# Moving two kinds of low-part subtraction from VectorE to GpSimd in the retention heads of an encoder kernel

## The reference, cut to what matters

```
h  = rmsnorm(x);  z = h @ w_in
y_ret = retention(rq, rk, rv, rg) @ w_ret_o        # 4 heads, dk 128, dv 256, both directions
   o = o * rsqrt(mean(o*o));  o = o * norm_g;  out = silu(g) * o
y_dil = dilated_attention(dq, dk, dv) @ w_dil_o    # 3 groups x 4 heads
x = x + (sigmoid(g_ret) * y_ret + sigmoid(g_dil) * y_dil) @ w_out
```

## Time and profile before

| | us |
|---|---|
| median of 3 runs (2579.22 to 2579.46) | 2579.38 |
| the profiled execution | 2579.25 |
| its span in the profile | 2577.4 |
| PE busy | 2569.2 |
| DVE busy | 1936.7 |
| ACT busy | 1120.5 |
| POOL busy | 128.3 |

### The profile page before, as it was taken

The page is one execution under the profiler, slowest core; times in us unless marked ns, Lnnn a source line. Parts: engine busy times, 40 slices in busy tenths (PEclk is TensorE's granted clock), DMA queues, the critical chain, the costliest instruction groups (busy, mean ns, idle before and its releaser), DMA issues.

```text
span 2577.4 us, 36835 instructions
## 1 busy us (share of the span) xinstructions
PE 2569.2 (100%) x14577; PEld 2255.8 (88%) x14577; DVE 1936.7 (75%) x2430; ACT 1120.5 (43%) x1369; POOL 128.3 (5%) x199
## 2 busy tenths in 40 slices
PE   9999999999999999999999999999999999999999
PEld 7999988888888888999989999888888888889998
DVE  8877866886776679777788777677867766797776
ACT  5433444445555234333443334444455542343332
POOL 1111000110001000000000000011100000000000
PEclk9999999999999999999999999999999999999999
DMA  5433245545443433333223332454554434333331
GB/s 183 149 124 119 66 142 192 174 159 175 138 138 115 163 101 120 101 103 98 99 83 123 98 98 74 174 177 147 172 155 138 138 126 153 115 115 98 102 107 53
DMA packets 201202, 328.98 MB, mean 128 GB/s; under 512 B 15572, under 2 KB 122497, under 8 KB 200525
## 3 DMA queue, kind: packets, MB, share of 16 engines
q1 hardware_dynamic: 186312, 286.35, 34.8%
q0 software_dynamic: 14112, 36.50, 3.9%
q10 hardware_dynamic: 646, 4.31, 0.4%
HBM read 289.11 MB, written 42.64 MB: 129 GB/s over the span
## 4 chain that ended last, share of the span: by engine, by line
PE 99%; DVE 1%; ACT 0%; DMA 0%; issue 0%; ACTq 0%
PE proj L692 23%; PE proj L694 23%; PE proj L693 23%; PE acc L692 9%; PE acc L693 9%; PE acc L694 9%; PE acc L1062 1%; PE acc L988 0%; PE acc L1011 0%; PE acc L970 0%; PE acc L971 0%; PE acc L1001 0%; PE acc L972 0%; PE acc L1000 0%; PE acc L765 0%; PE acc L759 0%
## 5 line engine op out<-in xcount | busy, mean ns | idle before, releaser
L692 PE MATMUL proj<-h_hi,ring_hi 128*128 128x256 f32 (+1 forms) x1632 | 553.4, 339 | 0.9 <-DVE h_lo L1788 0.8
L694 PE MATMUL proj<-h_hi,ring_lo 128*128 128x256 f32 (+1 forms) x1632 | 544.6, 334 | 0.0
L693 PE MATMUL proj<-h_lo,ring_hi 128*128 128x256 f32 (+1 forms) x1632 | 543.7, 333 | 0.0
L692 PE MATMUL proj<-y_hi,ring_hi 128*128 128x256 f32 (+1 forms) x1472 | 450.5, 306 | 0.0
L694 PE MATMUL proj<-y_hi,ring_lo 128*128 128x256 f32 (+1 forms) x1472 | 450.5, 306 | 0.0
L693 PE MATMUL proj<-y_lo,ring_hi 128*128 128x256 f32 (+1 forms) x1472 | 450.5, 306 | 0.0
L1262 ACT ACTIVATE ring_hi<-raw 128x1024 fp32r<-128x1024 f32 (+1 forms) x175 | 209.9, 1203 | 360.7 <-PE acc L694 194.6
L694 PEld LDWEIGHTS proj<-h_hi,ring_lo 128*128 128x128 f32 x1632 | 309.9, 190 | 31.2
L692 PEld LDWEIGHTS proj<-h_hi,ring_hi 128*128 128x128 f32 x1632 | 310.3, 190 | 30.3 <-DVE ring_lo L2569 1.2
L693 PEld LDWEIGHTS proj<-h_lo,ring_hi 128*128 128x128 f32 x1632 | 310.4, 190 | 27.5
L694 PEld LDWEIGHTS proj<-y_hi,ring_lo 128*128 128x128 f32 x1472 | 281.2, 191 | 12.5
(11 more groups left out here) (335 smaller groups left out, 4310.5 us busy)
## 6 DMA issues: line engine op xcount, KB each, us to landing
raw<-in_w_in SPq DMA_DIRECT2D x120, 512.0 KB, 4.7
raw<-in_ffn_gate SPq DMA_DIRECT2D x88, 512.0 KB, 3.7
raw<-in_ffn_up SPq DMA_DIRECT2D x88, 512.0 KB, 4.3
raw<-in_ffn_down SPq DMA_DIRECT2D x56, 512.0 KB, 4.4
qkv_d<-work POOLq DMA_DIRECT2D x72, 256.0 KB, 2.6
work<-in_ffn_down SPq DMA_DIRECT2D x32, 512.0 KB, 5.7
xs<-qkv_d SPq DMA_DIRECT2D x24, 512.0 KB, 6.3
xs<-in_w_in SPq DMA_DIRECT2D x16, 512.0 KB, 5.2
```

What stands on the lines that cost most here:

```text
L692: pe.matmul(o, s_hi, m_hi, start=start, stop=False, skip_group_check=onto)
L693: pe.matmul(o, s_hi, m_lo, start=False, stop=False, skip_group_check=onto)
L694: return pe.matmul(o, s_lo, m_hi, start=False, stop=stop, skip_group_check=onto)
```

## The change

GpSimd's program for a head gets three instructions between its fourth store and the wait for the squares: for n > 0 the two subtractions of `ret_low` of the head before, and for every n the low part of unit `at(4)`. VectorE loses the same instructions. VectorE's next weight splits (`at(1)` of heads 1 to 3 and `M_R0` in the merge) get a wait for GpSimd's increment of `weights_lo`, to keep the count in order.

```diff
@@ gpsimd head(l, n), behind the four stores of sigmoid tiles
+                if n:
+                    for e in (0, 1):
+                        pool.wait_ge(ret_hi, 2 * H - 1 + e)
+                        pool.tensor_tensor(y_lo[:, ds(2 * n - 2 + e, 1), :], ret_og[e].unsqueeze(1),
+                                           y_hi[:, ds(2 * n - 2 + e, 1), :].bitcast(fp32), ALU.subtract).then_inc(ret_lo, 1)
+                u = unit(l, HEAD_BASE + HEAD_UNITS * (n + 1))
+                pool.wait_ge(weights_hi, u.index + 1)
+                pool.wait_ge(weights_lo, u.index + LO_CREDIT)
+                pool.tensor_tensor(w_lo[u.slot], raw[:, u.slot, :], w_hi[u.slot].bitcast(fp32), ALU.subtract).then_inc(weights_lo, 1)
                 pool.wait_ge(ret_o_read, 4 * H + 2)
@@ vector
-            def split(u, n=2048):
+            def split(u, n=2048, behind_pool=False):
                 dve.wait_ge(weights_hi, u.index + 1)
+                if behind_pool:
+                    dve.wait_ge(weights_lo, u.index + LO_CREDIT)
                 dve.tensor_tensor(w_lo[u.slot][:, 0:n], raw[:, u.slot, 0:n], w_hi[u.slot][:, 0:n].bitcast(fp32),
                                   ALU.subtract).then_inc(weights_lo, 1)
@@ vector heads(l, n), n > 0
-                    split(at(1))
+                    split(at(1), behind_pool=True)
@@
                 reduce(3)
-                if n:
-                    ret_low(H - 1, n - 1)
                 ret_decay(H, 2)
@@
                 reduce(5)
-                split(at(4))
                 ret_decay(H, 3)
@@ vector merge(l)
-                split(at(M_R0))
+                split(at(M_R0), behind_pool=True)
```

## The result

The changed kernel takes 2589.19 us, median of 6 runs (2588.91 to 2589.38); the kernel before, beside it on the same chip, 2579.3 us (2579.17 to 2579.53). The ratio is 1.0038, 95% interval 1.0028 to 1.0049: slower by 9.9 us. 2590.0 had been forecast.

What follows compares the result with a forecast made beforehand. PE (TensorE) was taken as the bound; VectorE held behind GpSimd makes it wait 5.3 us a layer. 2579.25 + 10.6 = 2589.9, plus 0.13 for the median: 2590.0 us, own range 2584 to 2594.5, chance 0.50.

Steps and rivals of the forecast that it cites:

- PE is the bound, and relief of VectorE is worth 0: Whole kernel: TensorE busy 2569.2 of 2577.4 us, VectorE 75%; more VectorE slack gains 0 us.
- The unit's duration on GpSimd: Low part of `at(4)`, 2048 columns, as one GpSimd subtraction: 4.71 us taken, between 3.34 and 5.17.
- GpSimd first, VectorE held to its end: End of head 1: GpSimd starts at 696.9, scores_lo(2) at 697.36 and is held until 701.6.
- no change: Rival 1: engines share SBUF without blocking, 2579.4 us; chance 0.43 together with the first half of rival 3.
- The sum: PE's loss in heads 0 to 3: 1.4 + 1.6 + 1.6 + 0.7 = 5.3 us a layer, 10.6 for two.
- rv(3) decides in heads 0 to 2, rv(2) in head 3: PE late at rv(3) by 1.4, 1.6, 1.6 us in heads 0 to 2; at rv(2) by 0.7 in head 3.
- PE gets waits of 1 to 2 us: Sign of being right: PE waits at L692 for the low part, 1 to 2 us each, at rv(2) and rv(3).
- The moved DMA, `ret_lo`, the new waits: nothing: Load of `at(6)` and DMAs behind it 0.7 us later, `ret_lo` at 696.1, VectorE's new waits: all cost nothing.
- The reverse block: Rival 3: VectorE goes on, GpSimd is held: 2579.4 us (within 0.43), or about 2595 if slowed over threefold (0.04).

Runs made afterwards that it cites:

- the late kernel: Changed kernel, but GpSimd's unit waits until VectorE has scaled the next head's operands (head 3: until scores_lo(3)): 2579.25 us, ratio 1.0.
- the copies first: ScalarE's first two head-0 copies put ahead of at(3)'s high part: 2577.51 us on the kernel before, 2577.49 with the unit moved to GpSimd late.
- the four pieces: Changed kernel, but GpSimd's unit is four instructions of 512 columns, one behind the other: 2581.19 us, ratio 1.0007.
- the one input: Changed kernel, but GpSimd copies the unit twice with one input in place of the subtraction: 2579.35 us, ratio 1.0.
- the later start: Changed kernel, but GpSimd's unit waits until scores_lo(2) is done: 2584.75 us, ratio 1.0021.
- the one with memsets: Changed kernel, but GpSimd does three memsets of the unit's 2048 columns in place of the subtraction: 2581.98 us, ratio 1.0011.

## Why the prediction was right, point by point

- **PE is the bound, and relief of VectorE is worth 0.** Shown: with the whole change in place and no hold (the late kernel) 2579.25 us, and with the copies first no difference between moved and not moved.
- **The unit's duration on GpSimd.** 4.71 us was taken; it is 4.60 (36.8 us for 8), 0.11 below the term. The 4.50 us that the prediction cites from the Trainium skill, page "GPSIMD Engine Reference", section "Elementwise — side-by-side cycle accounting", for an addition lie 0.10 below what the subtraction took.
- **GpSimd first, VectorE held to its end.** Shown in all eight heads (four in each layer), and by the four pieces, the one input and the later start. The hold ended 0.14 us before what I counted (scores_lo(2) ends 0.55 us behind GpSimd, where its own duration is 0.69). Some luck was in the choice between this and "no change": the only row that spoke for a hold at all was a store's issue of 0.90 us in place of 0.54, and no run shows what lengthened that.
- **The sum.** Taken from the shift of PE's and VectorE's rows against before, in the first layer heads 0 to 3 lost 1.35 (0.04 of it ahead of the heads), 1.49, 1.51 and 0.53 us, 4.88 in all; 1.4, 1.6, 1.6 and 0.7 had been predicted, 5.3. PE's rv(3) in head 3 starts at 837.38 in place of 832.50, and the like in layer 1 at 2123.01 in place of 2113.35. The difference, 0.4 us a layer, is as much as the shorter unit gives (4 x 0.11), but other errors cancel beside it: in head 1 rv(3) starts only 1.36 us late (2.71 less the 1.35 of head 0) where 1.6 was counted, since the hold ended earlier too, and the matmuls behind the two hold-ups, which come late as well, make it 1.49. That last part had been left out of the sum.
- **rv(3) decides in heads 0 to 2, rv(2) in head 3.** Right for the totals. But "PE gets waits of 1 to 2 us" at both was wrong. At rv(2) of head 1 PE comes 1.10 us late (2.45 less 1.35) and the list shows 0.95. As PE is late already, rv(3) adds only 0.13, and the list shows none. In heads 0 to 2 the waits listed are 0.8 to 1.0 us, in head 3 it is 0.3.
- **The moved DMA, `ret_lo`, the new waits: nothing.** Right. SyncE's load of `at(6)`, at 700.88 before, was issued at 702.85, 0.6 us later against a head that itself came 1.35 late, and the unit could come 7.3 us later still at no cost.
- **The rival "no change"** (sharing without a block) had nearly as much chance as the forecast. It fell; the rows of before could not decide it, since no arithmetic of both engines overlaps there. **The reverse block** exists, but only for a GpSimd instruction that comes second (1754 ns in place of 1294 with four pieces, 2.24 us in place of 1.90 with two copies). In the changed kernel GpSimd is first in every head, and its unit takes 4.59 to 4.61 us throughout.
- **What the prediction missed.** The first instructions of the factors, TENSOR_SCALARs with one SBUF input, can also be held. In the changed kernel they come after GpSimd's end, so this costs nothing there; it makes the difference in the kernels with a later or a divided unit and in the one with memsets.

**What stays open.** No run puts the tensors elsewhere in SBUF, so it isn't excluded that their place matters. Against it: what was held read and wrote tensors other than GpSimd's, and memsets of the very buffer that the subtraction writes did not hold scores_lo(2).

The rule of the Trainium skill, page "SBUF — State Buffer", section "Who interferes with whom", is that of the prediction: the instruction that comes second waits for the end of the first. By the same section a GpSimd instruction that only writes doesn't count for two SBUF inputs, and a reduction never contends. The traces agree: two SBUF inputs against a reading GpSimd 4.67 us in place of 0.69, against a writing one 0.69; no reduction over 0.69; and the hold ends with each instruction. For the small TENSOR_SCALARs, which a memset did hold for 1.75 us, the same section says that such an instruction can enter a mode with two ports and contends then with any GpSimd operation; that these are in that mode no row shows.

## What to carry to other kernels

Before work is moved from VectorE to GpSimd, list which VectorE instructions will stand beside it and what inputs they have: one that takes two SBUF tensors and comes second waits for the end of GpSimd's reading instruction, and small TENSOR_SCALARs were held too. So the price is what is left of GpSimd's duration at that point, less the slack of what waits for VectorE. Put the GpSimd work into a stretch where VectorE pauses, reduces or reads PSUM, or cut it into pieces shorter than the slack. And first ask whether the engine that is relieved is one that the bound engine waits for; here it wasn't, and the best placement gave the time of before.

## What was not expected of the hardware

- A TENSOR_SCALAR of 24 float32 columns, SBUF to SBUF, 0.17 us by itself, took 2.26 us beside GpSimd's subtraction and 1.74 beside its memset; an int32 one took 1.75 beside the memset. A TENSOR_TENSOR of 512 columns took 0.69 beside the same kind of memset.
- VectorE's busy time counts the hold: 1942.3 us with 26.5 us of work less. Busy time that grows when work is removed is a sign of it; the duration by instruction (median 693, longest 4686 ns) shows where.
- Idle time of PE in the list of waits (5.9 us) was 60% of what was lost (9.9 us). Starts compared with those of before show 9.66 us of it by the end of the last head.
